# Splitting the first weight chunk earlier, over two engines, and computing the S5 poles one output tile later

## The chip, the cores and the metric
The kernel runs on one core of a Trainium2 chip. The metric is the device time of one execution in microseconds (us). The kernel before took 1642.92 us in the median of three runs (1642.27 to 1648.21).

## What is computed
Two transformer blocks on 512 tokens of width 1024, in float32. The first block begins as

```python
xn = rms_norm(h, norm_mix_pre)
proj = xn @ w_in          # qkv of a dilated attention, latents of an MLA, gates
```

and goes on with two attention mixers, a gate, an output projection and an MLP. The second block has four mixers (an S5 state space model among them), an output projection and a gated MLP. The S5 mixer needs the poles of its state space, small tables worked out from three parameters alone:

```python
dt = exp(log_dt); mag = exp(lr * dt)
ab_re = mag * cos(li * dt); ab_im = mag * sin(li * dt)
cf = (ab - 1) / (lr + i * li)
```

They depend on no activation, so they may be computed anywhere ahead of the second block.

## The kernel before
**Products.** Every matrix product is made of three passes with float32 operands split in a high and a low part: high by high, high by low, low by high (`products`, L242). So each weight must be split before TensorE can use it. The weights come in chunks of 128 partitions by up to 2048 columns (1 MB) through a ring of three slots. For each chunk SyncE issues the DMA (`issue_chunks`, L200), ScalarE rounds it into `ring_hi` (`split_hi`, L213), and VectorE subtracts to get `ring_lo`, which is written over the raw chunk (`split_lo`, L223). The semaphore `w_hi` counts high parts, `w_split` counts low parts; TensorE waits for `w_split` at the first use of a chunk (`wait_chunk`). A slot is filled again when TensorE is done with it.

**The first stage** (`stage_gemm` with `opening`, called at L1711) projects the normalised input: 25 output tiles. A group of four output tiles (one for each 128 tokens, t = 0 to 3) uses two chunks: four steps with the first half of the depth (chunk 0), then four with the second (chunk 1), and so on; output tiles 12 to 15 use chunks 6 and 7. A step is 12 matmuls of 512 columns. ScalarE evacuates the even output tiles from the PSUM bank and VectorE the odd ones (L636). Ahead of output tile j each of the two splits the chunks up to two past the one that finishes tile j, so at j = 12 chunks 7 and 8 are due. There are eight banks: tile j needs the one of tile j - 8 evacuated.

**The opening** (`Opening`, L273 to L422) stands ahead of that and makes the activations of four token tiles. For each token tile: ScalarE sums squares (`square`, L346), VectorE adds epsilon (`mean`, L381), GpSimd takes the power -1/2 (L373), VectorE scales (`scale`, L388), TensorE transposes into two banks (`turn`, L313), ScalarE rounds these to `xT_hi` (`high_part`, L352) and VectorE subtracts to `xT_lo` (`low_part`, L394). TensorE does `turn(0)`, `turn(1)`, step 0, `turn(2)`, step 1, `turn(3)`, steps 2 and 3, each step t waiting for `low_part(t)`. The order on each engine is written out by hand: on ScalarE `square(1)`, `square(2)`, `high_part(0)`, high part of chunk 0, `high_part(1)`, `square(3)`, high part of chunk 1; on VectorE `scale(1)`, `mean(2)`, `low_part(0)`, `scale(2)`, low part of chunk 0, `low_part(1)`, `mean(3)`, `scale(3)`, low part of chunk 1, `low_part(2)`, `low_part(3)`.

**The poles** (`s5_poles`, L2126) are hooked into the stage at output tile j = 12 (L420). ScalarE runs one Exp, waits for VectorE, runs one Exp and two Sin with a table load between them (L2136 to L2141). VectorE runs one instruction, waits for the first Exp, runs 11, waits for the last Sin, runs 15 more (L2146 to L2181), all of 128x8, most of them each waiting for the one before. Where the hook sits differs between the two engines:

```python
            for j in range(n):              # ScalarE
                split_hi(k, act, fin[j] + LEAD)
                if act_each is not None:
                    act_each(act, j)
...
            for j in range(n):              # VectorE
                if dve_each is not None:
                    dve_each(dve, j)
                split_lo(k, dve, fin[j] + LEAD)
```

So ScalarE reaches the poles behind its splits of tile j, VectorE ahead of them.

Of the kernel before, what the change touches and what calls it, by code (L numbers as in the profile page):

```python
# [21 lines left out]
ALU = mybir.AluOpType  # L22
# [25 lines left out]
CHUNK = 2048  # L48
# [17 lines left out]
class Signal:  # L66


    def __init__(self, sem):
        self.sem = sem  # L70
        self.base = 0
# [17 lines left out]
def plain(x):  # L89

    return x.bitcast(F32)
# [86 lines left out]
def col(k, name, i=0, n=1):  # L178
    a, _ = COLS[name]
    return k.cols[:, a + i:a + i + n]  # L180
# [23 lines left out]
def split_hi(k, act, upto):  # L204

    upto = min(upto, len(k.chunks))
    for g in range(k.hi_next, upto):
        n = k.chunks[g].n
        act.wait_ge(k.w_landed[g % SLOTS].sem, k.chunks[g].landed)
        if g >= SLOTS:  # L210
            sem, count = k.freed[g - SLOTS]
            act.wait_ge(sem, count)
        k.nc.scalar.copy(k.ring.hi[:, g % SLOTS, 0:n], k.raw[:, g % SLOTS, 0:n]).then_inc(k.w_hi.sem, 1)  # L213
    k.hi_next = max(k.hi_next, upto)


def split_lo(k, dve, upto):

    upto = min(upto, len(k.chunks))
    for g in range(k.lo_next, upto):  # L220
        n = k.chunks[g].n
        dve.wait_ge(k.w_hi.sem, g + 1)
        k.nc.vector.tensor_tensor(k.ring.lo[:, g % SLOTS, 0:n], k.raw[:, g % SLOTS, 0:n],  # L223
                                  plain(k.ring.hi[:, g % SLOTS, 0:n]), ALU.subtract).then_inc(k.w_split.sem, 1)
    k.lo_next = max(k.lo_next, upto)


def wait_chunk(k, pe, g):

    pe.wait_ge(k.w_split.sem, g + 1)  # L230
# [42 lines left out]
class Opening:  # L273
# [4 lines left out]
    def __init__(self, k, at):  # L278
        self.k = k
        self.gain = k.sb("op_gain", at[0], [P, D])  # L280
        self.xn = k.sb("op_xn", at[1], [P, 2, D])
        self.junk = k.sb("op_junk", at[2], [P, D])
        self.poles_act, self.poles_dve = s5_poles(k)
        self.ms, self.rs, self.half = k.stat[:, 0:2 * T], k.stat[:, 2 * T:3 * T], k.stat[:, 3 * T:3 * T + 1]
        (self.cols_in, self.ident_in, self.spread, self.gained, self.sumsq, self.mean, self.root, self.scaled, self.turned,
         self.high, self.low) = (k.sig("op_" + n) for n in (
             "cols", "ident", "spread", "gained", "sumsq", "mean", "root", "scaled", "turned", "high", "low"))

    def banks(self, t):
        return [self.k.pb[4 + t % 2 * 2 + c] for c in range(2)]  # L290
# [15 lines left out]
    def turn(self, pe, t):  # L306
        k = self.k
        if t >= 2:

            pe.wait_ge(self.low.sem, self.low.base + 2 * (t - 2) + 2)  # L310
        pe.wait_ge(self.scaled.sem, self.scaled.base + t + 1)
        for f in range(KD):
            mm = k.nc.tensor.transpose(self.banks(t)[f // 4][:, f % 4 * P:f % 4 * P + P],  # L313
                                       self.xn[:, t % 2, f * P:(f + 1) * P], k.ident[:, :])
            if f % 4 == 3:
                mm.then_inc(self.turned.sem, 1)

    def pe(self, pe, t):

        k = self.k  # L320
        if t == 0:
            pe.wait_ge(self.cols_in.sem, 16)
            pe.wait_ge(self.ident_in.sem, 16)
            for f in range(KD):
                mm = k.nc.tensor.transpose(k.pb[f // 4][:, f % 4 * P:f % 4 * P + P],
                                           col(k, "mix_pre", f).to_broadcast([P, P]), k.ident[:, :])
                if f % 4 == 3:
                    mm.then_inc(self.spread.sem, 1)
            self.turn(pe, 0)
        if t + 1 < T:  # L330
            self.turn(pe, t + 1)
        if t == 0:
            pe.wait_ge(self.gained.sem, 2)
        pe.wait_ge(self.low.sem, self.low.base + 2 * t + 2)

    def act(self, act):
        k, nc = self.k, self.k.nc
        act.dma_start(k.cols[:, :], k.d["cols"]).then_inc(self.cols_in.sem, 16)
        act.dma_start(k.ident[:, :], k.d["ident"]).then_inc(self.ident_in.sem, 16)

        def square(t):
            act.wait_ge(k.x_in[t].sem, 16)
            if t:

                act.wait_ge(self.sumsq.sem, self.sumsq.base + t)
            nc.scalar.activation(self.junk[:, :], k.h[:, t, :], ACT.Square, scale=1.0 / 32,  # L346
                                 accum_out=self.ms[:, t:t + 1]).then_inc(self.sumsq.sem, 1)

        def high_part(t):
            for c in range(2):  # L350
                act.wait_ge(self.turned.sem, self.turned.base + 2 * t + c + 1)
                nc.scalar.copy(k.xT.hi[:, 4 * c:4 * c + 4, t * P:(t + 1) * P],  # L352
                               self.banks(t)[c][:, :].rearrange("p (f e) -> p f e", f=4)).then_inc(self.high.sem, 1)

        square(0)
        for c in range(2):

            act.wait_ge(self.spread.sem, c + 1)
            nc.scalar.copy(self.gain[:, 512 * c:512 * c + 512], k.pb[c][:, :]).then_inc(self.gained.sem, 1)
        square(1)  # L360
        square(2)
        high_part(0)
        split_hi(k, act, 1)
        high_part(1)
        square(3)
        split_hi(k, act, 2)
        high_part(2)
        high_part(3)

    def pool(self, pool):  # L370
        for t in range(T):
            pool.wait_ge(self.mean.sem, self.mean.base + t + 1)
            self.k.nc.gpsimd.tensor_tensor(self.rs[:, t:t + 1], self.ms[:, T + t:T + t + 1], self.half,  # L373
                                           ALU.pow).then_inc(self.root.sem, 1)

    def dve(self, dve):
        k, v = self.k, self.k.nc.vector

        def mean(t):
            dve.wait_ge(self.sumsq.sem, self.sumsq.base + t + 1)  # L380
            v.tensor_scalar(self.ms[:, T + t:T + t + 1], self.ms[:, t:t + 1], EPS, None, ALU.add).then_inc(self.mean.sem, 1)  # L381

        def scale(t):
            dve.wait_ge(self.root.sem, self.root.base + t + 1)
            if t >= 2:

                dve.wait_ge(self.turned.sem, self.turned.base + 2 * (t - 1))
            v.scalar_tensor_tensor(out=self.xn[:, t % 2, :], in0=k.h[:, t, :], scalar=self.rs[:, t:t + 1],  # L388
                                   in1=self.gain[:, :], op0=ALU.mult, op1=ALU.mult).then_inc(self.scaled.sem, 1)

        def low_part(t):
            for c in range(2):
                dve.wait_ge(self.high.sem, self.high.base + 2 * t + c + 1)
                v.tensor_tensor(k.xT.lo[:, 4 * c:4 * c + 4, t * P:(t + 1) * P],  # L394
                                self.banks(t)[c][:, :].rearrange("p (f e) -> p f e", f=4),
                                plain(k.xT.hi[:, 4 * c:4 * c + 4, t * P:(t + 1) * P]),
                                ALU.subtract).then_inc(self.low.sem, 1)

        Chain(dve, k.sig("dve_chain"))(v.memset(self.half, -0.5))
        mean(0)  # L400
        dve.wait_ge(self.gained.sem, 2)
        scale(0)
        mean(1)
        scale(1)
        mean(2)
        low_part(0)
        scale(2)
        split_lo(k, dve, 1)
        low_part(1)
        mean(3)  # L410
        scale(3)
        split_lo(k, dve, 2)
        low_part(2)
        low_part(3)

    def poles(self, who):

        def each(eng, j):
            if j == 12:
                (self.poles_act if who == "act" else self.poles_dve)(eng)  # L420

        return each  # L422


def stage_norm_T(k, tag, src, width, gain, dst, xn_kb, arrive=None, sync=None):
# [7 lines left out]
    with nc.Block() as block:  # L433
# [19 lines left out]
        @block.gpsimd  # L453
        def _(pool):

            pool.wait_ge(root.sem, root.base + 1)
            nc.gpsimd.tensor_tensor(rs, ms, half, ALU.pow).then_inc(root.sem, 1)
# [53 lines left out]
def stage_gemm(k, steps, evac, owner=None, act_each=None, dve_each=None, dve_tail=None, pool=None,  # L511
# [25 lines left out]
    with nc.Block() as block:  # L537
# [83 lines left out]
        @block.gpsimd  # L621
        def _(eng):
            if opening is not None:
                opening.pool(eng)
            if pool is not None:
                pool(eng)
            if closing is not None:
                closing.pool(eng)
# [636 lines left out]
class Closing:  # L1265
# [181 lines left out]
    def high_part(self, act, t):  # L1447
        for c in range(2):
            act.wait_ge(self.turned.sem, self.turned.base + 2 * t + c + 1)
            self.k.nc.scalar.copy(self.k.xT.hi[:, 4 * c:4 * c + 4, t * P:(t + 1) * P],  # L1450
                                  self.bank(t, c)[:, :].rearrange("p (f e) -> p f e", f=4)).then_inc(self.high.sem, 1)
# [2089 lines left out]
```

## Time and profile before

| what | value |
|---|---|
| median of the runs | 1642.92 us |
| time of the profiled execution | 1641.97 us |
| its span, first to last instruction | 1640.2 us |
| TensorE busy | 1531.1 us (93% of the span) |
| VectorE busy | 809.4 us (49%) |
| ScalarE busy | 575.8 us (35%) |
| GpSimd busy | 282.6 us (17%) |
| mean granted TensorE clock | 0.956 |

The profiled execution's own time is 1.8 us above its span, and 0.95 us under the median of the runs. Busy shares are of the whole span; the change touches only about the first 110 us of it. A row of the timeline gives start, length, engine, line, operation, what it writes and reads, and in brackets how long the engine was idle before it and what released it. The granted clock is a share of TensorE's 2.4 GHz; 0.50 is its lower level, 1.2 GHz.

### The profile page before, as it was taken

The page shows a single profiled execution, that of the slowest core. Times are in us where ns is not written, and L with a number is a line of the kernel's source. Part 1 is how long each engine was busy: PE and PEld are TensorE (multiplying, and loading weights), DVE is VectorE, ACT ScalarE, POOL GpSimd, SP SyncE. Part 2 cuts the span into 40 slices and gives each one's busy share as a digit, 9 for nine tenths or more (in the row PEclk, how much of TensorE's full clock was granted, in tenths as well). Part 3 has the DMA queues.
Part 4 walks back from the last instruction along what each step waited for, and adds up shares of the span by engine and source line. Part 5 has one row for each costly group of instructions (what it writes and reads, how often), then busy time and mean ns, then how long its engine had stood idle before and what let it go on. Part 6 is the DMA issues. An engine that isn't in the chain of part 4 may idle for free. (4 is left out here: it accounts for less than half of the span.)

```text
span 1640.2 us, 18642 instructions
## 1 busy us (share of the span) xinstructions
PE 1531.1 (93%) x7560; PEld 1241.9 (76%) x7560; DVE 809.4 (49%) x1166; ACT 575.8 (35%) x902; POOL 282.6 (17%) x296
## 2 busy tenths in 40 slices
PE   7989699787999999999998999988799999999997
PEld 5878588685677888888886766766678888888885
DVE  4232433357756545434346786377755444324425
ACT  4221533435744433223235322285324222112212
POOL 0000000000032599000003265413222000000000
PEclk9999899789999999999999989989689999999998
DMA  4322121130022323322232212110012233222322
GB/s 174 103 78 80 52 78 46 45 104 26 2 85 93 105 92 103 103 90 90 103 128 62 77 53 77 58 52 27 1 52 77 78 103 103 102 80 100 103 90 77
DMA packets 38858, 129.25 MB, mean 79 GB/s; under 512 B 4676, under 2 KB 23004, under 8 KB 27380
## 3 DMA queue, kind: packets, MB, share of 16 engines
q1 hardware_dynamic: 38484, 127.93, 22.7%
q8 instruction: 60, 0.98, 0.2%
q14 instruction: 26, 0.21, 0.0%
q10 hardware_dynamic: 288, 0.12, 0.0%
HBM read 124.82 MB, written 3.17 MB: 78 GB/s over the span
## 5 line engine op out<-in xcount | busy, mean ns | idle before, releaser
L223 DVE TENSOR_TENSOR ring_lo<-ring_raw,ring_hi 128x2048 fp32r<-128x2048 f32 (+3 forms) x115 | 265.8, 2314 | 203.5 <-ACT ring_hi L213 203.4
L242 PE MATMUL bank<-xT_hi,ring_hi 128*128 128x512 f32 (+3 forms) x920 | 356.2, 387 | 5.9 <-DVE xT_lo L1570 4.7
L242 PE MATMUL bank<-xT_lo,ring_hi 128*128 128x512 f32 (+3 forms) x920 | 352.7, 383 | 0.0
L242 PE MATMUL bank<-xT_hi,ring_lo 128*128 128x512 f32 (+3 forms) x920 | 352.5, 383 | 0.0
L213 ACT CAST ring_hi<-ring_raw 128x2048 fp32r<-128x2048 f32 (+3 forms) x115 | 212.8, 1852 | 241.9 <-DMA ring_raw<-in_w_ff 131.1
L242 PEld LDWEIGHTS bank<-xT_hi,ring_hi 128*128 128x128 f32 (+2 forms) x920 | 174.1, 189 | 47.4 <-issue 7.6
L242 PEld LDWEIGHTS bank<-xT_hi,ring_lo 128*128 128x128 f32 (+2 forms) x920 | 174.0, 189 | 34.3
L242 PEld LDWEIGHTS bank<-xT_lo,ring_hi 128*128 128x128 f32 (+2 forms) x920 | 174.2, 189 | 33.1
L242 PE MATMUL bank<-ring_hi,hid_hi 128*128 128x512 f32 x432 | 169.6, 393 | 3.8 <-DVE ring_lo L223 3.8
L242 PE MATMUL bank<-ring_hi,hid_lo 128*128 128x512 f32 x432 | 169.1, 391 | 0.0
L242 PE MATMUL bank<-ring_lo,hid_hi 128*128 128x512 f32 x432 | 169.0, 391 | 0.0
L1495 POOL TENSOR_TENSOR stat<-stat 128x1 f32<-128x1 f32 x28 | 18.3, 655 | 653.1 <-DVE stat L1536 653.1
L242 PE MATMUL bank<-ring_hi,xT_hi 128*128 128x512 f32 (+1 forms) x288 | 108.0, 375 | 11.2 <-DVE ring_lo L223 8.9
L242 PE MATMUL bank<-ring_lo,xT_hi 128*128 128x512 f32 (+1 forms) x288 | 106.6, 370 | 0.0
L242 PE MATMUL bank<-ring_hi,xT_lo 128*128 128x512 f32 (+1 forms) x288 | 106.5, 370 | 0.0
L242 PEld LDWEIGHTS bank<-ring_hi,hid_hi 128*128 128x128 f32 x432 | 81.8, 189 | 21.2 <-DVE ring_lo L223 4.2
L242 PEld LDWEIGHTS bank<-ring_lo,hid_hi 128*128 128x128 f32 x432 | 81.9, 189 | 16.9
L242 PEld LDWEIGHTS bank<-ring_hi,hid_lo 128*128 128x128 f32 x432 | 81.7, 189 | 17.1
L242 PEld LDWEIGHTS bank<-ring_hi,xT_hi 128*128 128x128 f32 x288 | 59.0, 205 | 21.9 <-DVE ring_lo L223 6.2
L242 PEld LDWEIGHTS bank<-ring_lo,xT_hi 128*128 128x128 f32 x288 | 59.1, 205 | 7.5
L242 PEld LDWEIGHTS bank<-ring_hi,xT_lo 128*128 128x128 f32 x288 | 58.8, 204 | 7.9
L1855 POOL TENSOR_TENSOR gated_a<-gated_a,gated_b 128x512 f32<-128x512 f32 x8 | 13.0, 1635 | 300.1 <-DVE gated_b L1849 300.1
(496 smaller groups left out, 2157.8 us busy)
## 6 DMA issues: line engine op xcount, KB each, us to landing
ring_raw<-in_w_ff SPq DMA_DIRECT2D x30, 1024.0 KB, 4.9
ring_raw<-in_w_up SPq DMA_DIRECT2D x22, 1024.0 KB, 4.9
ring_raw<-in_w_proj SPq DMA_DIRECT2D x8, 1024.0 KB, 5.2
ring_raw<-in_w_gates SPq DMA_DIRECT2D x8, 1024.0 KB, 4.9
ring_raw<-in_w_fm SPq DMA_DIRECT2D x12, 512.0 KB, 4.7
ring_raw<-in_w_dn_a SPq DMA_DIRECT2D x6, 1024.0 KB, 4.8
ring_raw<-in_w_proj SPq DMA_DIRECT2D x8, 512.0 KB, 4.5
ring_raw<-in_w_out SPq DMA_DIRECT2D x4, 1024.0 KB, 4.9
```

The lines of the kernel that those rows point to most:

```text
L213: k.nc.scalar.copy(k.ring.hi[:, g % SLOTS, 0:n], k.raw[:, g % SLOTS, 0:n]).then_inc(k.w_hi.sem, 1)
L223: k.nc.vector.tensor_tensor(k.ring.lo[:, g % SLOTS, 0:n], k.raw[:, g % SLOTS, 0:n], plain(k.ring.hi[:, g % SLOTS, 0:n]), ALU.subtract).the ...
L242: mm = k.nc.tensor.matmul(out, x, y, start=first and n == 0, stop=last and n == 3 * len(pairs) - 1)
L1495: g.tensor_tensor(self.rs[:, x:x + 1], self.ms[:, 16 + x:17 + x], self.half, ALU.pow).then_inc(self.root.sem, 1)
L1855: nc.gpsimd.tensor_tensor(ga[:, f, :], ga[:, f, :], gb[:, f % 2, :], ALU.add).then_inc(summed.sem, 1)
```

## The change
In the opening, chunk 0 is split earlier. ScalarE rounds it behind `square(1)`, ahead of `high_part(0)` and `square(2)`, and these two change places. The low part of chunk 0 is made by two instructions of half the columns: VectorE does the first half behind `scale(1)`, ahead of `low_part(0)`, `mean(2)` and `scale(2)`; GpSimd does the second ahead of its power for token tile 2. TensorE waits for GpSimd's half by a new semaphore ahead of step 0. `low_part(0)` also moves ahead of `mean(2)`. The hook of the poles moves from output tile 12 to 13 on both engines; tile 13 has no chunk of its own to split.

```diff
@@ Opening.pe
         if t == 0:
             pe.wait_ge(self.gained.sem, 2)
+            pe.wait_ge(self.low_pool.sem, 1)
         pe.wait_ge(self.low.sem, self.low.base + 2 * t + 2)
@@ Opening.act
         square(1)
+        split_hi(k, act, 1)
+        high_part(0)
         square(2)
-        high_part(0)
-        split_hi(k, act, 1)
         high_part(1)
         square(3)
         split_hi(k, act, 2)
@@ new, and Opening.pool
+    def low_half(self, eng, half):
+        k, n = self.k, CHUNK // 2
+        at = slice(half * n, half * n + n)
+        return eng.tensor_tensor(k.ring.lo[:, 0, at], k.raw[:, 0, at], plain(k.ring.hi[:, 0, at]), ALU.subtract)
+
     def pool(self, pool):
         for t in range(T):
+            if t == 2:
+
+                pool.wait_ge(self.k.w_hi.sem, 1)
+                self.low_half(self.k.nc.gpsimd, 1).then_inc(self.low_pool.sem, 1)
             pool.wait_ge(self.mean.sem, self.mean.base + t + 1)
@@ Opening.dve
         scale(1)
+
+        dve.wait_ge(k.w_hi.sem, 1)
+        self.low_half(v, 0).then_inc(k.w_split.sem, 1)
+        k.lo_next = 1
+        low_part(0)
         mean(2)
-        low_part(0)
         scale(2)
-        split_lo(k, dve, 1)
         low_part(1)
@@ Opening.poles
-            if j == 12:
+            if j == 13:
                 (self.poles_act if who == "act" else self.poles_dve)(eng)
```

## Rows read from the trace of the kernel before

**Rows 1.** The page's first section, TensorE's line

```profile
PE 1531.1 (93%) x7560; PEld 1241.9 (76%) x7560; DVE 809.4 (49%) x1166; ACT 575.8 (35%) x902; POOL 282.6 (17%) x296
```

**Rows 2.** Waits of PE in 0 to 170 us: total, times, longest

```profile
PE bank L242 <- DVE ring_lo L223: 8.9, 2, 5.7
```

**Rows 3.** Timeline, output tiles 3, 4, 11, 12 and the poles

```profile
42.67 0.69 DVE L636 COPY qkA<-bank 128x512 f32<-128x512 f32 x1 [4.75 <-PE bank L242]
...
86.19 0.69 DVE L636 COPY qkA<-bank 128x512 f32<-128x512 f32 x1 [4.75 <-PE bank L242]
...
94.14 0.17 DVE L2149 TENSOR_TENSOR s_small<-s_small 128x8 f32<-128x8 f32 x1 [7.18 <-ACT s_small L2136]
...
100.34 0.17 DVE L2181 TENSOR_TENSOR s_small<-s_small 128x8 f32<-128x8 f32 x1
100.42 4.49 DVE L223 TENSOR_TENSOR ring_lo<-ring_raw,ring_hi 128x2048 fp32r<-128x2048 f32 x2
...
56.27 0.59 ACT L636 COPY qkA<-bank 128x512 f32<-128x512 f32 x1 [6.80 <-PE bank L242]
...
83.95 1.91 ACT L213 CAST ring_hi<-ring_raw 128x2048 fp32r<-128x2048 f32 x1
92.02 1.91 ACT L213 CAST ring_hi<-ring_raw 128x2048 fp32r<-128x2048 f32 x1 [6.15 <-DMA ring_raw<-in_w_proj]
93.83 0.20 ACT L2136 ACTIVATE s_small<-cols 128x8 f32<-128x8 f32 x1
...
107.20 0.37 ACT L636 COPY vA<-bank 128x256 f32<-128x256 f32 x1 [9.13 <-PE bank L242]
...
102.76 0.79 PE L242 MATMUL bank<-ring_hi,xT_hi 128*128 128x512 f32 x1 [5.73 <-DVE ring_lo L223]
```

**Rows 4.** Timeline of the opening, by engine, from 10 us

```profile
10.20 1.06 ACT L346 ACTIVATE op_junk<-h 128x1024 f32<-128x1024 f32 x1
...
12.92 1.90 ACT L213 CAST ring_hi<-ring_raw 128x2048 fp32r<-128x2048 f32 x1
14.72 1.08 ACT L352 CAST xT_hi<-bank 128x512 fp32r<-128x512 f32 x2
...
13.67 1.28 DVE L388 SCALAR_TENSOR_TENSOR op_xn<-h,stat,op_gain 128x1024 f32<-128x1024 f32 x1
14.86 2.29 DVE L223 TENSOR_TENSOR ring_lo<-ring_raw,ring_hi 128x2048 fp32r<-128x2048 f32 x1
17.07 1.28 DVE L394 TENSOR_TENSOR xT_lo<-bank,xT_hi 128x512 fp32r<-128x512 f32 x2
18.27 0.14 DVE L381 TENSOR_SCALAR stat<-stat 128x1 f32<-128x1 f32 x1
19.07 1.28 DVE L388 SCALAR_TENSOR_TENSOR op_xn<-h,stat,op_gain 128x1024 f32<-128x1024 f32 x1 [0.66 <-POOL stat L373]
20.27 2.29 DVE L223 TENSOR_TENSOR ring_lo<-ring_raw,ring_hi 128x2048 fp32r<-128x2048 f32 x1
22.87 1.29 DVE L394 TENSOR_TENSOR xT_lo<-bank,xT_hi 128x512 fp32r<-128x512 f32 x2 [0.32 <-ACT xT_hi L352]
...
17.30 0.77 PE L242 MATMUL bank<-ring_hi,xT_hi 128*128 128x512 f32 x1 [3.19 <-DVE ring_lo L223]
...
26.02 0.47 PE L242 MATMUL bank<-ring_hi,xT_hi 128*128 128x512 f32 x1
```

**Rows 5.** DMA issues at 2.6 us (chunk 0): KB, us to landing

```profile
ring_raw<-in_w_proj SPq DMA_DIRECT2D x1, 1024.0 KB, 8.6
```

**Rows 6.** Groups of POOL with 128x1024 operands: busy us, mean ns

```profile
L2263 POOL TENSOR_TENSOR s_er<-s_tmp 128x1024 f32<-128x1024 f32 x2 | 7.1, 3526 | 0.2
...
L2963 POOL TENSOR_TENSOR s5T_lo<-s_sg,s5T_hi 128x1024 fp32r<-128x1024 f32 x1 | 2.4, 2361 | 0.0
...
L2261 POOL TENSOR_TENSOR s_tmp<-s_er,s_small 128x1024 f32<-128x1024 f32 x2 | 3.8, 1896 | 0.2
```

**Rows 7.** Stretches: PE, PEld, DVE, ACT, POOL busy, PEclk, DMA share, GB/s

```profile
310.60:331.00 20.40, 15.77 (x78) 13.56 (x79) 7.78 (x17) 6.85 (x22) 0.00 (x0) 0.50 0.00 0
...
14.20:17.30 3.10, 0.01 (x1) 0.04 (x1) 3.10 (x3) 3.10 (x6) 0.00 (x0) 0.96 1.03 328
17.30:20.40 3.10, 3.10 (x7) 2.45 (x8) 2.44 (x5) 1.33 (x1) 0.54 (x1) 0.50 0.10 31
102.70:105.80 3.10, 3.04 (x7) 2.46 (x8) 2.21 (x2) 0.00 (x0) 0.00 (x0) 0.50 0.00 0
```

More of the change, by code:

```diff
@@ L285, in __init__ @@
         (self.cols_in, self.ident_in, self.spread, self.gained, self.sumsq, self.mean, self.root, self.scaled, self.turned,
-         self.high, self.low) = (k.sig("op_" + n) for n in (
-             "cols", "ident", "spread", "gained", "sumsq", "mean", "root", "scaled", "turned", "high", "low"))
+         self.high, self.low, self.low_pool) = (k.sig("op_" + n) for n in (
+             "cols", "ident", "spread", "gained", "sumsq", "mean", "root", "scaled", "turned", "high", "low", "low_pool"))
     def banks(self, t):
```

## The prediction

> **What bounds the kernel now.** Look first at the busy shares: TensorE works 93% of the span, the next engine 49% [rows 1]. So other engines matter only where TensorE stands still, and the next view is its waits in the first stage. One kind is touched by the change: TensorE waits twice, 8.9 us together, for a low part that VectorE makes [rows 2]. The timeline places both. The first is 3.19 us ahead of step 0, at 17.30 [rows 4]. The second is 5.73 us ahead of chunk 7, at 102.76 [rows 3].
>
> The second has a plain cause. Chunk 7's high part was done at 85.9 (83.95 + 1.91), and VectorE was free at 86.9, behind tile 11 (86.19 + 0.69). But it entered the poles first, and their second instruction there waited for ScalarE's Exp. That Exp stood behind the high part of chunk 8, which waited 6.15 us for its transfer and ran at 92.02. So VectorE idled 7.18 us, ended the poles at 100.5, and only then made the low parts of chunks 7 and 8 in 4.49 us [rows 3]. The split that TensorE wanted was queued behind small work that waited for the next chunk's DMA.
>
> **Part one, the poles one tile later.** At tile 12 VectorE now goes straight to the splits. Chunk 7: start 86.9, 2.29 us (the length of a full low part [rows 4]), ready at 89.2. TensorE wants it 5.73 us ahead of 102.76, at 97.0, so it is ready 7.8 us early. Chunk 8's low part follows its high part, 93.9 to 96.2, a chunk's time ahead of its use.
>
> What is the stall worth? I take it from outputs, not from the wait alone. Tile 3 leaves at 42.67 and tile 4 at 56.27, a step of 13.60 us between groups of four. From tile 11 to tile 12 the same work takes 107.20 - 86.19 = 21.01 us [rows 3]. The difference is **7.41 us**. The wait is 5.73 of it; the other 1.68 is mostly the clock, which was granted at 0.50 (1.2 GHz) for the 3.1 us behind the restart [rows 7]. Without the idle time TensorE keeps its clock there.
>
> Where do the poles go? Tile 12's evacuation no longer stands behind them on ScalarE, and nothing waits for them in this stage. TensorE would end tile 12 at 107.20 - 7.41 = 99.8; ScalarE copies it (two copies of 256 columns, under 1 us), so Exp starts near 100.6. From Exp to VectorE's last pole instruction took 100.51 - 93.83 = 6.7 us [rows 3], so both are done by 107.3. Queued behind them on VectorE is the evacuation of tile 13, due near 102.5 and so some 5 us late. Its waiter is tile 21, which needs that bank, over one more group of 13.60 + 8.16 us away: no cost. On ScalarE tile 14 is due near 105.3; its last Sin ended 2.2 us ahead of VectorE's end before, so it is met. The next low parts, chunks 9 and 10, are due at tile 16, behind these. SyncE's and GpSimd's queues are not passed by the poles, and no DMA moves in order. Table load and instruction counts are the same (5 on ScalarE with the load, 27 on VectorE). Bounds: 5.73 if the clock's part came back in another form, 7.41 if all of it goes. I take 7.41, since the clock's fall follows from the idle time, and that is gone.
>
> **Part two, chunk 0 earlier.** Chunk 0 was issued at 2.61 and landed 8.6 us later, at 11.2 [rows 5]. `square(1)` is over by 10.2 [rows 4], so ScalarE now waits about 1.1 us for the landing. That is new idle time, and it moves `high_part(0)` and `square(2)` back. The high part runs 11.25 to 13.15 (1.90), against 12.92 to 14.82: **1.7 us** earlier [rows 4].
> - ScalarE then: `high_part(0)` 13.1 to 14.2 (1.08 for two), `square(2)` to 15.3 (1.06 and its read-out), `high_part(1)` to 16.3, `square(3)` to 17.5, high part of chunk 1 to 19.3.
> - VectorE: free at 12.4, waits for the high part, first half of the low part from 13.2. The trace has no such subtraction of 1024 columns on VectorE; the bounds are half of 2.29, 1.15, and the scaling of 1024 columns, 1.28. I take 1.25, to 14.4. `low_part(0)` 14.4 to 15.7 (1.28).
> - GpSimd: second half from 13.2. Three groups of its 128x1024 subtractions and products last 1.90, 2.36 and 3.53 us on average [rows 6]. The one of 2.36 is the same form (subtract into a split's low part), so I take it: 13.2 to 15.6.
>
> So step 0 can start at about 15.8 against 17.30, **1.5 us earlier**, with VectorE and GpSimd arriving together. If GpSimd takes 1.90, VectorE decides and nothing changes; if 3.53, step 0 starts at 16.8.
>
> Does it last? VectorE and GpSimd now do `mean(2)`, the power, and `scale(2)` in series behind it. From a mean's start to its scale's start is 0.80 us (18.27 to 19.07). So: mean 15.7, `scale(2)` 16.5 to 17.8, `low_part(1)` 17.7 to 19.0, `mean(3)` 18.9, against 18.27 before, that is **0.6 us later**. From there the order is the old one: `scale(3)`, low part of chunk 1, `low_part(2)`. Before, `low_part(2)` could have begun at 22.5, when the split of chunk 1 ended, and waited 0.32 for ScalarE. Now it begins near 23.1 and ends at 24.4. TensorE began step 2 at 26.02, 8.72 us behind step 0; by itself it would come there at 15.8 + 8.7 = 24.5. The two chains meet: the gain at step 2 is 26.02 - 24.5 = **1.5 us**, and it is no larger even if TensorE runs step 0 faster. GpSimd at 3.53 delays the power, and all behind it, by 0.9: step 2 at 25.4, a gain of 0.6. Step 3 and chunk 1 have over 1 us of cover.
>
> The clock bears on this. It was still mostly high between the transposes and step 0 and at 0.50 just behind, for 3.1 us [rows 7]; with a gap of 1.7 instead of 3.2 us it may never fall. This would bring step 0 up to 1.6 us forward, but step 2 then waits for `low_part(2)` as worked out, so I add nothing.
>
> A new neighbour is that both halves of the low part read two SBUF operands at once, on VectorE and on GpSimd. The 3.53 us row is my upper end for that. The Trainium skill (GPSIMD Engine Reference, 1. Specifications) says that GpSimd's SBUF interfaces are shared with VectorE and contended when VectorE's instruction has two SBUF inputs. By it GpSimd's half would wait out up to VectorE's 1.25 us, last 3.6, and the change would gain 0.6 us here rather than 1.5; no run so far shows the overlap itself.
>
> **Sum.** 7.4 + 1.5 = 8.9 us. Against the profiled execution: 1641.97 - 8.9 = 1633.1, span 1631.3. That execution lies 0.95 under the median, so the median should come to 1642.92 - 8.9 = **1634.0 us**. TensorE-bound work and its loads, released by TensorE, all shift with it, so nothing takes the gain back directly. What a measurement of this kernel can tell from no change is about 0.5%, 8.2 us: the forecast lies just past that line.
>
> **Rivals.**
> - *A, forecast*: both parts land within 1.5 us of their price, or more. 1634.0. Chance 0.57.
> - *B, GpSimd late*: its half lasts 3.5 us or more beside VectorE's. Gain 7.4 + 0.6 = 8.0, time 1634.9. For it: the 3.53 row, and the power for tile 2 is queued behind it. Against: the same form ran in 2.36. Chance 0.20.
> - *C, given back at the clock*: 9 us earlier, the later stages meet the clock's changes at other points. Gaps restart at 0.50 for 3.1 us in the two shown, about 1.6 us each; losing two of these leaves a gain near 5.5, time 1637.4. For it: the mean clock differs by stretch, and one stretch of 20.4 us stayed at 0.50 with TensorE busy for 15.77 [rows 7]. Against: it may as well win. Chance 0.14. The Trainium skill (TensorE: Matmul & The Clock Gate, What's actually happening) says that the monitor behind the clock runs free of the kernel's start; by it the phase would vary between runs too and C would average out.
> - *D, the change does half*: the stall at chunk 7 stays in part, because its high part or its transfer is late in turn. Only a wait past 97.0 would show; there are 7.8 us of cover. Gain 1.5 to 4, time 1640. Chance 0.06.
> - *E, slower*: one more stretch such as the one at 310 us, entered after a gap, stays at 0.50. TensorE's 15.77 us there would have been half at 2.4 GHz if bound by columns, so each one costs up to 8. It decides only if it costs more than the 8.9 gained, as with a stretch of over 18 us of busy time: about 1644, and beyond 0.5% only if it is twice that. Chance 0.03.
>
> **Numbers.** A and part of B lie on either side of 8.2 us. A reaches from 7.5 to 12 us gained and has most of its weight past 8.2; with a little from C, which can also win, faster by over 0.5% gets 0.57, within 0.5% gets 0.42 (half of that from B and A's lower edge), slower 0.01. The range takes A and B and C's centre: 1630.5 (3.5 us more, should the clock's changes fall well) to 1638.0.
>
> **What would show it.** Right: no wait of TensorE for `ring_lo` near 97; from tile 11's to tile 12's output 13.6 us; low part of chunk 7 at about 85.4, poles ending near 105.8 (both 1.5 us less than the times above, by the opening); ScalarE waiting for chunk 0's transfer until 11.2; step 0 at 15.8 and step 2 at 24.5. GpSimd's half at 2.4 us says A, at 3.5 says B. A gap ahead of step 2 says that VectorE's chain is the longer one. Wrong: a span shortened much less than tile 12's output moved (C, E), or a wait for chunk 7 that stays (D).

## The result, and the profile after

The changed kernel took **1633.64 us** in the median of 7 runs (1628.02 to 1637.95), the kernel before 1642.68 in 7 runs. The ratio is 0.9946, with a 95% interval of 0.9926 to 0.9965: 0.54% less, and the line of 0.5% that the forecast named lies inside the interval. The forecast was 1634.0. The profiled execution took 1632.75 us, with a span of 1631.0 (1640.2 before). Busy shares hardly moved; what went is idle time of TensorE. Its waits in 0 to 170 us now name no VectorE low part (columns: total, times, longest; [rows 2] before):

```profile
PE bank L1260 <- DVE qkA L1275: 11.9, 1, 11.9
PE bank L325 <- DMA ident<-in_ident: 6.5, 1, 6.5
PE bank L242 <- POOL ring_lo L374: 2.2, 1, 2.2
PE bank L313 <- DVE op_xn L398: 2.0, 1, 2.0
```

The 5.7 us at chunk 7 are gone. The first line belongs to the next stage: this wait is in the profile before too (11.8 us), but there it ends behind 170 us. Ahead of step 0 TensorE waits for a new partner, GpSimd. The timelines of VectorE and ScalarE around output tiles 11 to 13 answer to [rows 3]:

```profile
85.57 0.69 DVE L649 COPY qkA<-bank 128x512 f32<-128x512 f32 x1 [4.75 <-PE bank L242]
86.18 2.28 DVE L223 TENSOR_TENSOR ring_lo<-ring_raw,ring_hi 128x2048 fp32r<-128x2048 f32 x1
93.42 2.29 DVE L223 TENSOR_TENSOR ring_lo<-ring_raw,ring_hi 128x2048 fp32r<-128x2048 f32 x1 [4.96 <-ACT ring_hi L213]
95.63 0.16 DVE L2159 TENSOR_SCALAR s_small<-cols 128x8 f32<-128x8 f32 x1
100.03 0.17 DVE L2162 TENSOR_TENSOR s_small<-s_small 128x8 f32<-128x8 f32 x1 [4.24 <-ACT s_small L2149]
...
106.24 0.17 DVE L2194 TENSOR_TENSOR s_small<-s_small 128x8 f32<-128x8 f32 x1
106.32 0.42 DVE L649 COPY vA<-bank 128x256 f32<-128x256 f32 x1
...
91.48 1.91 ACT L213 CAST ring_hi<-ring_raw 128x2048 fp32r<-128x2048 f32 x1 [6.23 <-DMA ring_raw<-in_w_proj]
99.17 0.37 ACT L649 COPY vA<-bank 128x256 f32<-128x256 f32 x1 [5.78 <-PE bank L242]
```

Chunk 7's low part starts at 86.18 instead of 100.42 and is ready at 88.5. Tile 12 follows tile 11 by 99.17 - 85.57 = 13.60 us, where it was 21.01: the stall of 7.41 us is wholly gone. TensorE's granted clock was 1.00 from 95 to 100 us, where no gap broke it up any more. VectorE still waits 4.24 us inside the poles, but now nobody waits for VectorE. Tile 13's evacuation starts at 106.32, over 4 us late, without a waiter.

The opening answers to [rows 4] (timeline of the changed kernel, all engines, in order of time):

```profile
11.08 1.90 ACT L213 CAST ring_hi<-ring_raw 128x2048 fp32r<-128x2048 f32 x1 [0.99 <-DMA ring_raw<-in_w_proj]
...
13.02 1.23 DVE L374 TENSOR_TENSOR ring_lo<-ring_raw,ring_hi 128x1024 fp32r<-128x1024 f32 x1 [0.64 <-ACT ring_hi L213]
13.06 3.40 POOL L374 TENSOR_TENSOR ring_lo<-ring_raw,ring_hi 128x1024 fp32r<-128x1024 f32 x1 [2.00 <-ACT ring_hi L213]
...
14.16 1.28 DVE L404 TENSOR_TENSOR xT_lo<-bank,xT_hi 128x512 fp32r<-128x512 f32 x2
...
15.36 0.15 DVE L391 TENSOR_SCALAR stat<-stat 128x1 f32<-128x1 f32 x1
...
16.42 0.53 POOL L383 TENSOR_TENSOR stat<-stat 128x1 f32<-128x1 f32 x1
16.56 0.47 PE L242 MATMUL bank<-ring_hi,xT_hi 128*128 128x512 f32 x1 [2.15 <-POOL ring_lo L374]
...
16.99 1.28 DVE L398 SCALAR_TENSOR_TENSOR op_xn<-h,stat,op_gain 128x1024 f32<-128x1024 f32 x1 [1.49 <-POOL stat L383]
...
24.65 1.03 PE L313 MATMUL bank<-ident,op_xn 128*128 128x128 f32 x8
...
25.44 0.48 PE L242 MATMUL bank<-ring_hi,xT_hi 128*128 128x512 f32 x1
```

GpSimd's half took 3.40 us, not 2.36. Step 0 starts at 16.56 (17.30 before) and step 2 at 25.44 (26.02). Step 2 did not wait for VectorE: `low_part(2)` ran from 23.60 to 24.88. Tile 12's output is 107.20 - 99.17 = 8.03 us earlier, and so is the stage's last one. The span is 9.2 us shorter. So 1.2 us came from behind the first stage, where no instruction was changed.

Three questions were put to experiments. Is the stall a matter of the queue's order? What slows GpSimd? Does the opening's part reach the total at all?

### The profile page after: what moved, and what is told of

Read it like the earlier page. It is cut to its first block and busy times, and to the rows that moved or that the text cites. A ratio compares the mean times of both kernels' runs of the same rounds, so it can differ in the third digit from the quotient of the medians.

```text
span 1631.0 us, 18644 instructions
## 1 busy us (share of the span) xinstructions
PE 1531.7 (94%) x7560; PEld 1243.0 (76%) x7560; DVE 811.3 (50%) x1166; ACT 575.9 (35%) x902; POOL 287.8 (18%) x297
## 5 line engine op out<-in xcount | busy, mean ns | idle before, releaser
L223 DVE TENSOR_TENSOR ring_lo<-ring_raw,ring_hi 128x2048 fp32r<-128x2048 f32 (+4 forms) x114 | 262.8, 2307 | 201.3 <-ACT ring_hi L213 201.2
L242 PEld LDWEIGHTS bank<-ring_hi,hid_lo 128*128 128x128 f32 x432 | 81.6, 189 | 17.2
L242 PEld LDWEIGHTS bank<-ring_lo,hid_hi 128*128 128x128 f32 x432 | 81.8, 189 | 16.9
```

The costliest lines, as they stand in the source:

```text
L242: mm = k.nc.tensor.matmul(out, x, y, start=first and n == 0, stop=last and n == 3 * len(pairs) - 1)
```

## The experiments

### The poles alone (e1, e12), the opening alone (e2)

```diff
# e1 and e12: the kernel before
-            if j == 12:
+            if j == 13:
# e2: the changed kernel
-            if j == 13:
+            if j == 12:
```

> The kernel before, with the poles hooked in at output tile 13 and the old opening. Theory (the stall at chunk 7 is a queue order, worth 7.4 us): step 2 stays at 26.0, tile 12's output comes at 99.8 instead of 107.20, no wait of TensorE for ring_lo behind the opening, total 1642.7 - 7.4 = 1635.3, give or take 2 from later stages. Rival (the two parts lean on each other, the whole 9 us comes from both): tile 12 at 101 or later, total above 1638.

> The changed kernel with the poles back at output tile 12. Theory: the new opening is worth 0.6 us at step 2 (25.44 as in the changed kernel), and the stall at chunk 7 is back in full, since it hangs on chunk 8's transfer, which moves with TensorE: tile 12's output at 106.6, total 1642.1. Rival (the opening is worth more downstream than its 0.6 us, which would explain why the whole gained 9.0 and the first stage only 8.0): total 1641.0 or less with tile 12 at 106.6.

| kernel | median us (runs) | ratio to before, 95% | step 0 | step 2 | tile 11 to 12 | tile 12 |
|---|---|---|---|---|---|---|
| e1, poles alone | 1632.82 (6) | 0.9939, 0.9916 to 0.9963 | 17.20 | 26.95 | 13.60 | 100.69 |
| e2, opening alone | 1642.37 (12) | 0.9998, 0.9984 to 1.0011 | 16.64 | 25.47 | 21.09 | 106.73 |

The kernel before took 1642.78 us beside them (17 runs). The poles alone bring all of the gain that can be measured, the opening alone none: its interval reaches from 2.6 us faster to 1.8 us slower, so a gain of 0.6 us can't be told from nothing here. In e2 the stall is back whole, as TensorE's row and the total of its waits show:

```profile
102.03 0.80 PE L242 MATMUL bank<-ring_hi,xT_hi 128*128 128x512 f32 x1 [5.55 <-DVE ring_lo L223]
...
PE bank L242 <- DVE ring_lo L223: 5.6, 1, 5.6
```

e1 missed its forecast in two places. Its total was expected at 1635.3, give or take 2, and came at 1632.82: 9.96 us below the kernel before, where the stall is worth 7.41. This returns below, in the account of the total. And tile 12's output came at 100.69 instead of 99.8. Its opening is that of the kernel before, yet step 2 came at 26.95 instead of 26.02. All 12 matmuls of its step 0 ran at the lower clock, 0.43 us apart, where before the last four were already 0.23 apart (timeline of TensorE, e1):

```profile
21.18 0.63 PE L242 MATMUL bank<-ring_hi,xT_hi 128*128 128x512 f32 x1
21.60 0.63 PE L242 MATMUL bank<-ring_lo,xT_hi 128*128 128x512 f32 x1
22.03 0.63 PE L242 MATMUL bank<-ring_hi,xT_lo 128*128 128x512 f32 x1
...
23.64 0.39 PE L242 MATMUL bank<-ring_lo,xT_hi 128*128 128x512 f32 x1
23.87 0.40 PE L242 MATMUL bank<-ring_hi,xT_lo 128*128 128x512 f32 x1
```

So one opening gives different times in different executions, by nearly a microsecond. That is more than the 0.58 us that the new opening gained in the first pair of traces.

### The order of two items in VectorE's queue (e3)

```diff
             for j in range(n):
+                if opening is not None:
+                    split_lo(k, dve, fin[j] + LEAD)
                 if dve_each is not None:
                     dve_each(dve, j)
                 split_lo(k, dve, fin[j] + LEAD)
```

> The kernel before, poles still at output tile 12, but VectorE makes the low parts of tile 12 ahead of its poles, the order ScalarE has already. Theory (what cost was that the low part of chunk 7 stood behind the poles): TensorE does not wait near 97, tile 12's output at 99.8 to 100.3, the same as at tile 13. Rival (the poles cost by their length on ScalarE and VectorE, wherever in tile 12 they stand): tile 12 at 104 or later.

The poles stay at tile 12, and TensorE's only wait for a low part in this stage was the 2.9 us ahead of step 0. The total was 1633.34 us in one run. Tile 12's output came at 101.01, later than expected. Step 2 was at 26.61 in this execution, which carries 0.59 of it. The other 0.66 is ScalarE's: tile 11 to 12 was 14.26 us, because tile 12's evacuation stood behind the poles' last Sin (ScalarE's timeline, e3):

```profile
94.63 0.20 ACT L2138 ACTIVATE s_small<-cols 128x8 f32<-128x8 f32 x1
99.28 0.21 ACT L2141 ACTIVATE s_small<-s_small 128x8 f32<-128x8 f32 x1 [4.45 <-DVE s_small L2165]
...
100.92 0.19 ACT L2143 ACTIVATE s_small<-s_small 128x8 f32<-128x8 f32 x1
101.01 0.35 ACT L638 COPY vA<-bank 128x256 f32<-128x256 f32 x1
```

That delay reached nobody: the stage's last output came 71.63 us behind tile 11, exactly as in e1 (158.38 - 86.75 and 158.72 - 87.09). So the stall hung on the order of two entries in one queue. For the stall, the length of the poles and the tile they stand at did not matter.

### Are the poles free at tile 13? (e8)

```diff
-            if j == 13:
+            if j == 17:
```

> The changed kernel with the poles at output tile 17 instead of 13, beside another group of tiles. Theory (at 13 the poles cost nothing any more: tile 13's late output has no waiter): tile 12's output at 99.2 and the first stage's last output within 0.2 us of the changed kernel's. Rival (the poles at 13 still cost, by the late evacuation of tile 13 and the splits of chunks 9 and 10 behind it): the last output comes earlier by 0.5 us or more.

Tile 12 came at 99.22 and the stage's last output at 157.25, in the changed kernel at 99.17 and 157.21. At tile 13 the poles cost the stage nothing, by one profile of each. The total of its one run was 1631.57 us, inside the scatter.

### What slows GpSimd (e4, e5, e6, e9)

Four variants of the changed kernel: all of the low part on VectorE (e4), GpSimd first and VectorE idle meanwhile (e5), 1536 columns against 512 (e6), and beside GpSimd only `low_part(0)`, which reads one operand from PSUM (e9).

```diff
# e4: the low part by VectorE alone (GpSimd's half and TensorE's wait for it left out)
-        dve.wait_ge(k.w_hi.sem, 1)
-        self.low_half(v, 0).then_inc(k.w_split.sem, 1)
-        k.lo_next = 1
+        split_lo(k, dve, 1)
# e5: VectorE begins when GpSimd has ended
         dve.wait_ge(k.w_hi.sem, 1)
+        dve.wait_ge(self.low_pool.sem, 1)
         self.low_half(v, 0).then_inc(k.w_split.sem, 1)
# e6
-        k, n = self.k, CHUNK // 2
-        at = slice(half * n, half * n + n)
+        k, n = self.k, 1536
+        at = slice(n, CHUNK) if half else slice(0, n)
# e9: as e5, with low_part(0) first
+        low_part(0)
         dve.wait_ge(k.w_hi.sem, 1)
+        dve.wait_ge(self.low_pool.sem, 1)
         self.low_half(v, 0).then_inc(k.w_split.sem, 1)
         k.lo_next = 1
-        low_part(0)
```

> The changed kernel, with the whole low part of chunk 0 on VectorE at its early place and nothing of it on GpSimd. If GpSimd's half is slow because VectorE runs beside it (3.40 us against 2.36 elsewhere), two engines bring next to nothing: low part 13.0 to 15.3, low_part(0) to 16.5, step 0 at 16.6 (16.56 in the changed kernel), power of tile 2 no longer queued behind the half, so scale(2) at 17.2 against 16.99, step 2 at 25.5 to 25.7 against 25.44. Rival (the split over two engines is what brings the gain): step 0 at 17.0 or later and step 2 at 26.0.

> The changed kernel, but VectorE begins its half of chunk 0's low part only when GpSimd has ended its own, so that GpSimd runs with VectorE idle. Theory (VectorE's reading two operands beside it slows GpSimd): GpSimd's half takes 2.3 to 2.5 us instead of 3.40. Rival (3.4 us is what this subtraction takes on GpSimd at this place, say because of the transfers that land meanwhile): 3.3 us or more. Step 0 comes at 18.0 to 18.1 by the theory (13.06 + 2.36, then 1.23 and 1.28), at 19.1 by the rival.

> The changed kernel with three quarters of chunk 0's low part (1536 columns) on VectorE and one quarter (512) on GpSimd. VectorE: 1.75 us from 13.0, then low_part(0) to 16.05. GpSimd: alone, 512 columns would take some 1.2 to 1.6 us; if it loses VectorE's two-operand time beside it, up to 2.5. Either way it ends by 15.6, ahead of low_part(0), so step 0 at 16.1 to 16.2 against 16.56, and step 2 at 25.2 to 25.5, as the mean and power of tile 2 now wait for VectorE. If GpSimd is still the last to end, step 0 at 16.5 or later.

> The changed kernel with low_part(0) ahead of VectorE's half, and that half only once GpSimd's has ended. So beside GpSimd's half VectorE reads one operand from PSUM and one from SBUF, for 1.28 us, and no instruction with two SBUF operands. Theory (GpSimd loses time to VectorE's two SBUF operands, and to nothing else of VectorE's): its half takes 2.3 to 2.5 us, step 0 at 16.8 to 16.9. Rival (any work of VectorE beside it slows it): 2.9 us or more, step 0 at 17.3 or later.

GpSimd's part in the timelines of e5, e6, e7 (below) and e9, in this order, each as start, length, operation and shape:

```profile
13.16 2.35 POOL L374 TENSOR_TENSOR ring_lo<-ring_raw,ring_hi 128x1024 fp32r<-128x1024 f32 x1 [2.00 <-ACT ring_hi L213]
```

```profile
13.15 2.84 POOL L374 TENSOR_TENSOR ring_lo<-ring_raw,ring_hi 128x512 fp32r<-128x512 f32 x1 [2.00 <-ACT ring_hi L213]
```

```profile
13.21 3.12 POOL L374 TENSOR_TENSOR ring_lo<-ring_raw,ring_hi 128x768 fp32r<-128x768 f32 x1
```

```profile
13.14 2.36 POOL L374 TENSOR_TENSOR ring_lo<-ring_raw,ring_hi 128x1024 fp32r<-128x1024 f32 x1 [2.08 <-ACT ring_hi L213]
```

And what VectorE did beside it in e9, for 1.29 us inside GpSimd's 2.36:

```profile
13.58 1.29 DVE L404 TENSOR_TENSOR xT_lo<-bank,xT_hi 128x512 fp32r<-128x512 f32 x2 [1.20 <-ACT xT_hi L353]
```

With VectorE idle the half takes 2.35 us, and beside an instruction that reads PSUM and SBUF 2.36. Beside VectorE's own half, with two SBUF operands for 1.23 us, it takes 3.40: 1.05 more. In e6 half the columns took *longer* than all 1024 did alone, 2.84 us, since VectorE read two SBUF operands for 1.76 us beside it. What 512 columns take without such a neighbour is in the profile before: another subtraction of that shape took 1.29 us, beside a VectorE copy out of PSUM. By it the added time in e6 is 1.55 us. For the 768 columns of e7 an estimate half way between 1.29 and 2.35 is 1.82, and 3.12 - 1.82 = 1.30 were added beside VectorE's 1.49. So in all three cases GpSimd lost 85% to 88% of VectorE's time, all but 0.2 us of it, and VectorE paid nothing: its half took 1.23 us beside GpSimd and 1.23 alone (e5, e9).

The profile before, which was at hand for the prediction, holds that row and shows the slowing too, in later stages (timelines of GpSimd and then VectorE):

```profile
617.52 1.29 POOL L2263 TENSOR_TENSOR s_er<-s_tmp 128x512 f32<-128x512 f32 x1
...
631.77 1.90 POOL L2264 TENSOR_TENSOR s_tmp<-s_er,s_small 128x1024 f32<-128x1024 f32 x1
633.63 3.94 POOL L2265 TENSOR_TENSOR s_tmp<-s_ei,s_small 128x1024 f32<-128x1024 f32 x1
...
1156.36 2.36 POOL L2963 TENSOR_TENSOR s5T_lo<-s_sg,s5T_hi 128x1024 fp32r<-128x1024 f32 x1
...
632.74 3.07 DVE L223 TENSOR_TENSOR ring_lo<-ring_raw,ring_hi 128x2048 fp32r<-128x2048 f32 x1 [3.30 <-ACT ring_hi L213]
...
1154.64 2.55 DVE L3006 COPY_PREDICATED hg_acc<-mask_lev,bank 128x512 f32<-128x512 uint16 x4
```

Two products of one shape took 1.90 and 3.94 us on GpSimd. The second began while VectorE was splitting a chunk, with two SBUF operands. That split had itself begun while the first was still running, and took 3.07 us where 2.29 is its length alone. The 2.36 of the prediction's row was measured beside VectorE instructions that read a PSUM bank, for its first 0.8 us, and with VectorE idle after that.

Hence e4: with no GpSimd at all, step 0 came at 16.65 against 16.56. The second engine brought 0.1 us there. The rival expected step 0 at 17.0 or later, and in this it falls. Step 2 was at 26.76 in e4, beyond both forecasts, again with all of step 0 at the lower clock. In e5 step 0 came at 18.30 and in e9 at 16.98, 0.2 and 0.1 us behind their forecasts. The one run of each took 1634.13 us (e4), 1639.96 (e5), 1632.96 (e6) and 1632.29 (e9).

e6 missed its numbers. GpSimd's quarter, forecast at 2.5 us at most and over by 15.6, ended at 15.99; step 0 came at 16.32 (forecast 16.1 to 16.2) and step 2 at 24.73 (25.2 to 25.5). But it shows the other chain. Its step 0 was not slowed by the clock, and `turn(3)` was through by 23.9. But step 2 started at 24.73 and waited for VectorE (TensorE's timeline, e6):

```profile
22.82 1.04 PE L313 MATMUL bank<-ident,op_xn 128*128 128x128 f32 x8
24.73 0.50 PE L242 MATMUL bank<-ring_hi,xT_hi 128*128 128x512 f32 x1 [0.87 <-DVE xT_lo L404]
```

### Two better openings (e7, e10), and the parts side by side (e11, e12)

```diff
# e7 and e10, ScalarE
         square(1)
+        square(2)
         split_hi(k, act, 1)
         high_part(0)
-        square(2)
# e7 and e10, VectorE: mean(2) behind scale(1), ahead of the low part
# e7: GpSimd's part behind the power of tile 2; 1280 columns on VectorE, 768 on GpSimd
# e10: no part on GpSimd, the whole low part on VectorE as in e4
```

> The changed kernel with three edits: the sum of squares of token tile 2 back ahead of chunk 0's high part on ScalarE (in the idle time before the transfer lands), its mean and power ahead of the low halves on VectorE and GpSimd, and 1280 columns on VectorE against 768 on GpSimd. Theory (VectorE's and GpSimd's chain to low_part(2) sets step 2): high part of chunk 0 at 11.4 (0.3 later), step 0 at 16.2 to 16.9, scale(2) right behind low_part(0) at 16.1, low_part(1) to 18.6, step 2 at 24.5 to 25.0 against 25.44, tile 12's output 98.3 to 98.7 against 99.17, total 0.5 to 1 us less than the changed kernel, which the timing can't tell for sure. Rival (TensorE's own chain sets step 2): step 2 follows step 0 by 8.7 to 8.9 us whatever VectorE does.

> The changed kernel without GpSimd's half: the whole low part of chunk 0 on VectorE at its early place, and the sum of squares of token tile 2 and its mean and power ahead of it. Theory (GpSimd's help is eaten by the contention, and what then counts is when scale(2) comes): high part at 11.4, low part 13.3 to 15.6, low_part(0) to 16.9, step 0 at 16.9 to 17.0, scale(2) right behind, so step 2 at 25.3 to 25.9 by TensorE's chain at the lower clock. In total no difference to the changed kernel that the timing can tell. Rival (two engines matter): total over 2 us above the changed kernel in this comparison.

> The changed kernel as it is, to stand beside the next one on the same chip. Theory: 9 us less than the kernel before, 1633 to 1634.5. The opening's part should be what it has over the next kernel: 0.6 us or a little more, too little to tell from the scatter of the later stages. Rival (the opening carries over a microsecond or two into the total): 1.5 us or more below the next kernel.

> The kernel before with only the poles moved to output tile 13, beside the full change on the same chip. Theory: 1633.5 to 1635.5, within a microsecond of the full change, no wait of TensorE for chunk 7. Rival: as above, 1.5 us or more above the full change.

| kernel | median us (runs) | ratio to before, 95% | step 0 | step 2 | tile 12 |
|---|---|---|---|---|---|
| e7 | 1631.82 (6) | 0.9919, 0.9896 to 0.9942 | 16.44 | 25.27 | 99.00 |
| e10 | 1630.41 (6) | 0.9929, 0.9903 to 0.9955 | 16.62 | 25.20 | 98.96 |
| e11, the full change | 1633.49 (8) | 0.9941, 0.9919 to 0.9962 | 16.84 | 26.60 | 100.34 |
| e12, the poles alone | 1633.43 (7) | 0.9943, 0.9921 to 0.9964 | 17.31 | 26.68 | 100.44 |

e7 missed: step 2 was to come at 24.5 to 25.0, and it followed step 0 by 8.83 us, as its rival said. VectorE's chain was short enough by then (`low_part(2)` ended at 24.02), and TensorE's own, with the low clock in it, decided. e10 had step 0 at 16.62 and step 2 at 25.20, both a little ahead of its forecast (16.9 to 17.0, and 25.3 to 25.9), with one engine fewer. Both were nominally a little faster than the changed kernel, but all intervals overlap: no version was shown to beat it.

e11 and e12 put the full change beside the poles alone: they came out 0.06 us apart in the median, each with an interval 7 us wide. Over all profiles, step 2 with the old opening came at 26.02, 26.95, 26.61 and 26.68 (mean 26.57), with the new one at 25.44, 25.47, 25.48 and 26.60 (mean 25.75). The means are 0.8 us apart, and one late profile (e11, whose opening began 0.28 us late and had all of step 0 at the lower clock) lies among those of the old opening. Such a gain is too little for the total to show.

The profiles of e11 and e12 are 7.2 us apart in span, with the same instructions from tile 12 on. Here is the stretch where they part, for the changed kernel's first profile (e11's has 909 matmuls at the same 0.80) and then for e12 (columns as in [rows 7]):

```profile
1100.00:1260.00 160.00, 143.78 (x908) 117.06 (x907) 102.42 (x177) 62.65 (x124) 45.52 (x34) 0.80 0.12 40
```

```profile
1100.00:1260.00 160.00, 138.08 (x950) 114.53 (x949) 108.25 (x182) 65.41 (x127) 46.20 (x34) 0.88 0.12 40
```

With a granted clock of 0.88 instead of 0.80, TensorE did 42 more matmuls there in less busy time. From the first stage's last output to the end took 1474.96 us in the profile before and 1473.79 after; over the twelve experiments it went from 1466.1 (e12) to 1479.2 (e5).

## Why the prediction was right or wrong

**The stall at chunk 7: right, to the hundredth.** Forecast 7.41 us from the steps between outputs, measured 21.01 - 13.60 = 7.41, and 21.09 against 13.60 in e2 and e1. Taking the price from outputs, not from the wait of 5.73, was what made it right. TensorE kept its clock (1.00), as argued. The poles' new place was free in the stage (e8), and the evacuation of tile 13 was about as late as foreseen. One small reading was off: ScalarE's last Sin ended 2.4 us ahead of VectorE's end, not 2.2; tile 14 was met all the same.

**The opening: right in its order of events, wrong in one term.** Chunk 0 landed at 11.1 and its high part ended at 13.0, against 11.2 and 13.15 forecast. VectorE's half took 1.23 for 1.25. The failed step is "The one of 2.36 is the same form (subtract into a split's low part), so I take it". The form was the same, but beside that row VectorE read a PSUM bank or stood idle, and beside the new half it reads two SBUF operands. It is not so either that no run had shown the overlap: the trace before had it at 633.63 us. Rival B was the nearer one: step 0 at 16.56, step 2 0.6 us earlier, and 8.0 us at tile 12. Its own line of 3.5 us was not quite reached, with 3.40. The rule on the shared interfaces that was weighed against the row (the Trainium skill, GPSIMD Engine Reference, 1. Specifications) was the better guide: 3.6 by it, 3.40 measured. e5 and e9 show that it holds for two SBUF operands and not for one beside PSUM.

**"The two chains meet": right as a bound, not what decided.** VectorE's chain does set step 2 when step 0 is quick (e6). In the changed kernel it ended at 24.88, and TensorE's own chain brought step 2 at 25.44, 8.88 us behind step 0 (8.72 before), with the clock falling inside step 0. Rival B had this 25.4 from VectorE's chain, so that the number fits is luck.

**The total: right, in good part by luck.** The forecast was 8.9 us, 7.4 for the poles and 1.5 for the opening; 9.04 came out in the medians. But the parts came out otherwise. The poles alone gave 9.96 (e1) and 9.30 (e12), and the opening nothing that can be told. Each interval taken alone still contains 7.4. The 13 runs of the poles alone and the 31 of the kernel before beside them have medians 9.35 us apart, with a 95% interval of about 8.4 to 11.4 by resampling these runs. So some 2 us of the gain arise behind the first stage.

The traces say the same. Behind the first stage the two kernels with the stall took 1475.0 and 1475.2 us (before, e2). Nine of the twelve profiles without it took 1472.6 to 1474.6; the others took 1466.1, 1475.4 and 1479.2. Followed along ScalarE, at the same instruction in both profiles, the changed kernel's lead over the one before was 7.0 us at 311.8 (times of the profile before), 9.0 at 406.4, 8.8 at 895.1, 11.0 at 1014.0, 15.0 at 1113.4, 8.1 at 1149.4 and 9.2 at the end. The first two rises, of about 2 us each, are in nine of the twelve profiles and not in e2. The last swing goes with the granted clock, here before and then after (columns as in [rows 7]):

```profile
1082.00:1113.00 31.00, 31.00 (x192) 25.96 (x190) 19.05 (x49) 24.80 (x40) 11.00 (x8) 0.83 0.20 69
1113.00:1150.00 37.00, 30.60 (x245) 23.36 (x243) 28.88 (x54) 18.93 (x45) 10.79 (x11) 0.95 0.09 30
```

```profile
1082.00:1113.00 31.00, 29.31 (x197) 24.47 (x195) 21.47 (x53) 22.28 (x39) 11.82 (x8) 1.00 0.27 93
1113.00:1150.00 37.00, 34.22 (x210) 26.49 (x211) 23.56 (x44) 15.35 (x46) 15.97 (x15) 0.51 0.02 9
```

This is rival C's mechanism, mostly with the other sign, and it does not average out as the argument beside C had it: part of it comes back from run to run. The rest is scatter. The executions of the changed kernel spread over 13 us (1625.07 to 1637.95, both batches). That the sum of 8.9 fits is therefore two misses that cancel: an opening priced too high, and a gain in later stages that had been put at nothing. Why the later stages gain was not tested.

D and E did not occur.

## What to carry to other kernels

When an engine waits inside small side work, look at what is queued behind it on that engine. Here, swapping two entries brought all of the gain that can be measured (9.4 us in e3's one run), and the second part of the change nothing measurable. Before a piece of work is given to GpSimd, ask what VectorE reads meanwhile: a price from a row holds only for the neighbours that it had there, and the trace shows these neighbours. Price a stall by the distance between outputs around it, since the restart at the lower clock is in that (7.41 us here) and not in the wait (5.73). And when a total comes out as forecast, check the parts: here two of them were off and cancelled.

## What had not been expected of the hardware

- GpSimd's subtraction stood nearly still while VectorE read two SBUF operands: 512 columns took 2.84 us beside 1.76 us of it, 1024 columns 2.35 alone.
- VectorE can pay too. In every case shown here the engine that began second paid; in the opening that was GpSimd, by 0.04 us (13.06 and 13.02). In e7 VectorE's scaling of 1024 columns, with two SBUF operands, began while GpSimd still ran to 16.33, and took 1.64 us instead of 1.28:

```profile
15.78 1.64 DVE L398 SCALAR_TENSOR_TENSOR op_xn<-h,stat,op_gain 128x1024 f32<-128x1024 f32 x1
```

- The granted clock in the profile is no proof of the level in the opening. In e1 it reads 1.00 over 17.2 to 20.4, while the matmuls were 0.43 us apart, twice the 0.23 of later ones (columns as in [rows 7]):

```profile
17.20:20.40 3.20, 3.20 (x8) 2.55 (x9) 2.54 (x5) 1.34 (x1) 0.54 (x1) 1.00 0.14 43
```

What stays open is why the clock's changes fall differently from one execution to the next, and why most executions without the stall gain some 2 us in later stages. No experiment was made on either.
